# Normalised rows stored as blocks of inner columns, and one instruction for an expert's output rows

## The reference

```python
x = x + gt1[:, None, :] * mix
h2 = modulate(rmsnorm(x, norm2_g[l]), sh2, sc2, dt)          # rows * root * gain + shift
...
def per_sequence(args):
    xs, cw = args
    a = jax.nn.silu(jnp.einsum('sd,edf->sef', xs, w_gate)) * jnp.einsum('sd,edf->sef', xs, w_up)
    return jnp.einsum('sef,efd->sd', a * cw[..., None], w_down)   # cw: two of 32 experts a token
...
x = x + gt2[:, None, :] * ffn
```

## Time and profile before

| | |
|---|---|
| median of 3 runs | 1054.54 us (1052.35 to 1054.55) |
| the profiled execution's own time | 1054.91 us |
| its span | 1053.1 us |
| PE, PEld busy | 979.8 (93%), 768.8 (73%) |
| DVE, ACT busy | 798.3 (76%), 529.1 (50%) |
| L1573, 128x1024, x8 | 1284 ns each |
| L1577, 128x1024, x8 | 1224 ns each |
| `xg_transposes`, L2218 | 256 matmuls |
| `y_evac`, L1795 and L1796 | 32 each, 686 and 677 ns |

### The profile page before, as it was taken

One profiled execution on the slowest core, in us unless ns is written; L12 is line 12 of the kernel. 1 busy time (PEld: TensorE's weight loads), 2 busy tenths in 40 slices (PEclk: granted clock), 3 DMA queues, 4 the chain that ended last, 5 costly groups with the idle time before them and its releaser, 6 DMA issues.

```text
span 1053.1 us, 15470 instructions
## 1 busy us (share of the span) xinstructions
PE 979.8 (93%) x5658; PEld 768.8 (73%) x5658; DVE 798.3 (76%) x1484; ACT 529.1 (50%) x929; POOL 109.4 (10%) x151
## 2 busy tenths in 40 slices
PE   3899988999999999999999999799999999999996
PEld 3668768987897998989988888366666666666642
DVE  8767758944894895967775768888888887777828
ACT  4545432653265465554653333266656656565532
POOL 0200101000100001010000000112211221212100
PEclk9699989999999999999999999899999999999998
DMA  9733423330333225230185434469999999999275
GB/s 365 240 96 119 136 91 91 112 100 22 109 93 101 66 72 164 62 101 1 42 321 185 180 139 182 175 251 367 371 364 366 374 363 359 361 354 347 98 308 210
DMA packets 81033, 206.78 MB, mean 196 GB/s; under 512 B 11878, under 2 KB 40630, under 8 KB 72780
## 3 DMA queue, kind: packets, MB, share of 16 engines
q1 hardware_dynamic: 59232, 156.25, 41.2%
q0 software_dynamic: 15120, 43.72, 13.0%
q10 hardware_dynamic: 6620, 6.00, 1.7%
HBM read 189.61 MB, written 24.71 MB: 204 GB/s over the span
## 4 chain that ended last, share of the span: by engine, by line
PE 60%; DVE 20%; DMA 11%; ACT 4%; issue 4%; SPq 0%; ACTq 0%; DVEq 0%
PE PS L1946 11%; PE PS L1948 10%; PE PS L1947 10%; DMA WGU<-in_w_exp_up 7%; PE PS L2227 4%; DMA AR<-in_w_ada 3%; PE PS L2013 3%; PE PS L2235 3%; PE PS L2234 3%; PE PS L2233 3%; DVE ACC L1253 3%; DVE AT L1427 3%; DVE WL L1318 2%; PE PS L2218 2%; PE PS L2337 1%
## 5 line engine op out<-in xcount | busy, mean ns | idle before, releaser
L1946 PE MATMUL PS<-WH,HT 128*128 128x256 f32 x512 | 147.1, 287 | 1.3 <-ACT GVH L919 1.3
L1947 PE MATMUL PS<-WL,HT 128*128 128x256 f32 x512 | 145.0, 283 | 0.0
L1948 PE MATMUL PS<-WH,HL 128*128 128x256 f32 x512 | 144.9, 283 | 0.0
L1783 DVE TENSOR_TENSOR WGL<-WGU,WGH 128x1024 fp32r<-128x1024 f32 x96 | 116.9, 1220 | 20.1 <-ACT WGH L1161 18.8
L1427 DVE COPY_PREDICATED AT<-MASK,PS 128x64 f32<-128x64 uint8 x320 | 72.7, 227 | 65.9 <-PE PS L2024 47.0
L1161 ACT ACTIVATE WGH<-WGU 128x1024 fp32r<-128x1024 f32 x96 | 98.6, 1064 | 40.5 <-DMA WGU<-in_w_exp_up 32.9
L1946 PEld LDWEIGHTS PS<-WH,HT 128*128 128x128 f32 x512 | 98.4, 192 | 4.0 <-issue 4.0
L1947 PEld LDWEIGHTS PS<-WL,HT 128*128 128x128 f32 x512 | 98.5, 192 | 0.0
L1948 PEld LDWEIGHTS PS<-WH,HL 128*128 128x128 f32 x512 | 98.3, 192 | 0.0
L2233 PE MATMUL PS<-WGH,XGTH 128*96 128x512 f32 x192 | 88.4, 461 | 0.0
L1821 DVE TENSOR_TENSOR WDL<-WDN,WDH 128x2048 fp32r<-128x2048 f32 x32 | 73.4, 2292 | 17.8 <-ACT WDH L1171 17.7
(11 more groups left out here) (349 smaller groups left out, 2248.2 us busy)
## 6 DMA issues: line engine op xcount, KB each, us to landing
WGU<-in_w_exp_gate SPq DMA_DIRECT2D x32, 1024.0 KB, 12.5
WGU<-in_w_exp_up SPq DMA_DIRECT2D x32, 1024.0 KB, 18.6
WDN<-in_w_exp_down SPq DMA_DIRECT2D x32, 1024.0 KB, 14.0
AR<-in_w_ada POOLq DMA_DIRECT2D x32, 512.0 KB, 4.5
WF<-in_w_in SPq DMA_DIRECT2D x28, 512.0 KB, 5.4
AST<-in_w_ada SPq DMA_DIRECT2D x16, 512.0 KB, 9.1
AR<-in_w_ada_final POOLq DMA_DIRECT2D x16, 512.0 KB, 4.4
YG<-expert_rows SPq DMA_DIRECT2D x8, 1024.0 KB, 13.3
```

What stands on the lines that cost most here:

```text
L1783: V.tensor_tensor(WGL[s][:, :, ks, :], WGU[s][:, :, ks, :], WGH[(NCH * s + c) % 4][:].bitcast(F32), ALU.subtract).then_inc(wgl_ready, 1)
L1946: MM(ps, wh, xh, start=first, stop=False)
L1947: MM(ps, wh, xl, start=False, stop=False)
L1948: return MM(ps, wl, xh, start=False, stop=last)
```

## The change

Three edits.

1. `XN` is written in another order of columns. In `rows_scaled` DVE still reads `X1` and `GS2B` contiguously, but writes with the inner dimension `k` at a distance of 128 elements (512 bytes): block `k` of a row then holds columns `k, k + 8, ...` side by side. `rows_shifted` reads and writes `XN` contiguously, and reads `SH2B` at a distance of 8 elements (32 bytes).
2. `xg_transposes` reads `k * P:(k + 1) * P` where it read `k::KD`. The stored and gathered rows have the same sizes, and what lands in PSUM is the same.
3. `y_evac` multiplies both halves in one instruction of 96x1024.

```diff
             def rows_scaled(t):
                 if t >= 2:
                     v_.wait_ge(xn_st[t % 2], 16 * (t // 2))
-                link(V.scalar_tensor_tensor(out=XN[:, t % 2, :], in0=X1[:, t, :], scalar=RR[:, t:t + 1], in1=GS2B[:],
-                                            op0=ALU.mult, op1=ALU.mult))
+                link(V.scalar_tensor_tensor(out=XN[:, t % 2, :].rearrange("p (k n) -> p n k", k=KD),
+                                            in0=X1[:, t, :].rearrange("p (n k) -> p n k", k=KD), scalar=RR[:, t:t + 1],
+                                            in1=GS2B[:].rearrange("p (n k) -> p n k", k=KD), op0=ALU.mult, op1=ALU.mult))
 
             def rows_shifted(t):
-                V.tensor_tensor(XN[:, t % 2, :], XN[:, t % 2, :], SH2B[:], ALU.add).then_inc(xn_ready, 1)
+                xn = XN[:, t % 2, :].rearrange("p (k n) -> p k n", k=KD)
+                V.tensor_tensor(xn, xn, SH2B[:].rearrange("p (n k) -> p k n", k=KD), ALU.add).then_inc(xn_ready, 1)
...
             def y_evac(par, done):
-                V.tensor_tensor(YB[0:C, par, 0:HALF], YP[par][0:C, 0:HALF], GT2B[0:C, 0:HALF], ALU.mult)
-                V.tensor_tensor(YB[0:C, par, HALF:D], YP[par][0:C, HALF:D], GT2B[0:C, HALF:D], ALU.mult).then_inc(done, 1)
+                V.tensor_tensor(halves(YB[0:C, par, :]), halves(YP[par][0:C, :]), halves(GT2B[0:C, :]), ALU.mult).then_inc(done, 1)
...
             def xg_transposes(slot, done):
                 for k in range(KD):
-                    last = TR(TP[:, k // 4, (k % 4) * C:(k % 4 + 1) * C], XG[0:C, slot, k::KD], IDENT[0:C, 0:C])
+                    last = TR(TP[:, k // 4, (k % 4) * C:(k % 4 + 1) * C], XG[0:C, slot, k * P:(k + 1) * P], IDENT[0:C, 0:C])
```

## The result

The changed kernel took 1059.09 us (median of 7 runs, 1057.74 to 1062.76), against 1053.19 us for the kernel before in the same jobs. The ratio is 1.0053, interval 1.0042 to 1.0064: 5.6 us slower (4.4 to 6.7). The profiled execution took 1061.27 us, its span 1059.4 us where it was 1053.1. Of these 6.3 us the first 1.9 are not the change's: `residual` of tile 0, ahead of which no instruction was touched, starts at 596.58 us, where it was 594.69 (in the thirteen traces of this document it starts anywhere from 593.64 to 597.61 us).

The account below looks back on a forecast made before the run. Full DMA load stream bounds the expert stage; PE, then DVE from tile 4, the rows stage. 1054.9 + 4.7 - 0.6 - 0.1 = 1058.9 us, as a median 1058.5, put at 1059.0; 8-in-10 range 1051.5 to 1064.0.

Parts of the forecast that it names:

- Both strides cost: Main case: on DVE the strided write of rows_scaled and strided read of rows_shifted each cost 0.75 us; chance 0.50.
- d: Extra DVE time per tile in the two rows instructions: 1.5 us, with bounds 0 and 2.15 us.
- How d adds up: Rows stage: each residual's delay is the previous one plus d, less DVE's waits, reaching 3.65 us at residual(7).
- The room of DVE: DVE's waits ahead of residual, which absorb delay: 1.84 us in tiles 2 to 4, 0.22 and 0.53 in 6 and 7.
- F: Delay at rows_shifted(7), carried into the start of the full DMA stream: 4.7 us, with bounds 1.5 and 9.9.
- PE's lateness in tile 7: PE's transposes of tile 7 come 3.65 less 0.45 us of room late, 3.20 us, and DVE waits for them.
- The gain in the expert stage: 0.6 us from transposes of the second and fourth sets, plus 0.1 us from merged y_evac in experts 30 and 31.
- The forecast's 0.28 us a step: PE's saving per set of eight contiguous transposes: 8 x 0.027 us from start distances plus 0.065 us.
- Only one stride: Rival: on DVE only the write or only the read costs; F = 1.5, gain 0.7, time 1055.3 us; chance 0.17.
- none: Rival: no stride costs on DVE; time 1053.8 us; chance 0.12.
- PE's saving coming through: Rival: DMAs serve more than 368 GB/s, expert stage ends 8.7 us earlier; time 1050.5 or 1047 us; chance 0.21.
- the stride costs nothing on PE: Rival: transposes save nothing, sum 0.6 us higher, 1059.6 us, not told apart by time; no chance given.

Follow-up runs that it names:

- only the write strided: Changed kernel with the shift row stored in block order beforehand, so rows_shifted is contiguous: ratio 1.0025, 2.6 us slower than the kernel before.
- rows instructions alone: Changed kernel with strided transposes and two y instructions again, leaving only the new rows instructions: ratio 1.0046, 4.9 us slower than the kernel before.
- the buffer given back early: Changed kernel with DVE's copy that frees PE's ranks buffer moved up in one_hots(0): ratio 1.0065 to the kernel before.
- transposes alone: Kernel before with only the transposes made contiguous, rows and y instructions as before: ratio 0.9999.
- one y instruction: Kernel before with only y_evac merged into one instruction: ratio 0.9998.
- two strided reads: Kernel before with rows_scaled writing contiguously and reading X1 and GS2B at 32 bytes: one execution, durations only, 1.02 us more than with no stride.
- 16 bytes: Kernel before with rows_scaled writing and rows_shifted reading the shift row at 16 bytes: one execution, durations only, 2.06 and 2.00 us.
- blocks by ACT: ACT copies X1 into XN in block order, DVE's rows instructions contiguous, transposes and y_evac as in the changed kernel: ratio 0.9996 to the kernel before.
- 8 bytes: Kernel before with rows_scaled writing and rows_shifted reading the shift row at 8 bytes: one execution, durations only, 1.28 and 1.23 us.
- the light pair: Kernel before and changed kernel, both loading only half the down weights of experts 4 to 31: ratios 0.9943 and 0.9927, medians 1048.78 and 1047.36 us.

## Why the prediction was right

**Both strides cost** was the case forecast, and both do. The price was d = 1.5 us a tile from a single row, 0.75 for each instruction. They measured 0.79 and 0.84, and from start of L1573 to the next `residual` a tile takes 4.07 us where it took 2.57 (601.05 - 598.48): 1.50 us, as forecast. That it comes to 1.50 and not to 0.79 + 0.84 is the overlap noted at the first profile lines. That one row of another operation gave it to 0.01 us is partly luck: by starts the write is above 0.75 and the read below. The choice to price the write like the read, for which no row stood, is shown right by the kernel with only the write strided.

**How d adds up.** Forecast for `residual(1)`, (2), (5), (6), (7): 1.5, 1.16, 1.69, 2.97, 3.65 us; measured 1.51, 1.21, 1.86, 3.18, 4.40. The room of DVE in each tile was what counted. The same arithmetic with one stride alone had given F = 1.5, and the kernel with only the write strided shows 1.6.

**The term that was too small is PE's lateness in tile 7.** The forecast let PE's transposes of tile 7 come 3.65 - 0.45 = 3.20 us late, with PE itself on time and at its old pace. They came 4.40 us late, and F was 5.9 us and not 4.7. Two things were left out. The first is a wait. PE had 2.96 us of room for the residual, but next to none for the ranks' buffer in tile 6, which stands behind `one_hots(0)` on the same DVE queue: before the change PE started 0.23 us after that copy ended, and now the transposes of tile 6 come 2.7 us late. The second is PE's pace behind the wait: at a granted clock of 0.64 and 0.51 the matmuls up to tile 7 lose another 1.7 us.

The trace of the rows instructions alone has the first without the second. The wait for the buffer is as long there, the clock stays at 1.00, and `residual(7)` does not wait for PE at all: the transposes of tile 7 come 3.44 us late, close to 3.20. So the wait for the buffer does not cost anything at `residual(7)` by itself; some 0.2 us of the 1.2 are sizes, and the other 1 us is, by this comparison of two traces, the lower clock. The kernels that escape it in tile 6 meet it one step later, in the logits of tile 7 (3.50 us, and 3.60 with the buffer given back early), where DVE waits for them 0.72 and 0.82 us: F is 5.6 in both.

**The gain in the expert stage** was put at 0.6 + 0.1 us. The two traces alone say 1.5, but single traces differ by as much with the same code in the stage (338.4 and 336.5 in the first column). All eleven full-load traces, the stage in us:

| transposes with stride | | contiguous transposes | |
|---|---|---|---|
| before | 338.4 | changed | 336.9 |
| rows alone | 336.2 | transposes alone | 335.9 |
| one y instruction | 337.6 | only the write strided | 338.6 |
| two strided reads | 336.8 | ranks' buffer early | 337.4 |
| 16 bytes | 336.5 | blocks by ACT | 337.2 |
| 8 bytes | 337.7 | | |
| mean | 337.2 | mean | 337.2 |

So the saving there is not to be told from nothing, with 2 to 3 us between traces of either kind, and the 0.7 us can't be confirmed or excluded. That DMAs, and not PE, set the stage's end is shown by the light pair, where the same edit is worth 6.2 us. The forecast's 0.28 us a step was 0.21: the two light kernels take 9.70 and 9.49 us a step. The part from the distance between starts, 8 x 0.027 = 0.22 us, is all that came; the 0.065 us added to it for the weight load did not.

**The sum.** Forecast 4.7 - 0.7 = 4.0 us, with 0.5 us more for the range's lopsidedness; measured 5.6 (4.4 to 6.7), with F at 5.9 in the trace. The 1.2 us that F was short are the larger part of the 1.6 between sum and measurement, and the rest is within the interval. That the median of 1059.09 us falls on the forecast of 1059.0 is luck: the kernel before had a median of 1053.19 in the same jobs, 1.4 us under the one that the forecast started from, and this made up for the term that was too small.

**Rivals.** Only one stride, none, and PE's saving coming through are excluded by the durations and by the transposes alone. That the stride costs nothing on PE is wrong as well (0.21 us a set), but as the forecast said, the time doesn't show it. One sign that the forecast had named against itself did appear: GB/s above 370 after 720 us, 372 and 377 in the changed kernel. The bound was set too close. The kernel before itself has 371 between 790 and 820 us, and at 372 and 377 GB/s PE still ran short of weights from the stretch after 820 us on, earlier than the 860 us named. The figure of 358 GB/s that the forecast sets beside the stretches is thus passed by about 5%. DVE's room in the expert stage is 3.6 to 6.2 us of 30 by the earlier trace rows, not 3 to 5; nothing hangs on it.

**Open.** Why the stage differs by 2 to 3 us between traces at DMA shares of 0.98 to 1.02 was not looked into. Nor is it shown why the clock fell in tile 6 behind a wait of 2.22 us in the changed kernel (and of 2.25 in its light version), and stayed at 1.00 behind one of 2.24 in the kernel with the rows instructions alone. In each of these traces the fall came behind waits of PE; no run tried the waits by themselves.

## What to carry to other kernels

Ask of a saving which stage it falls in and what that stage waits for: 0.2 us a step on an engine that is busy 100% was worth nothing that runs can show, because a queue with a growing latency stood behind it, and 6 us as soon as that queue had room. Put a stride where an engine waits anyway: the reordering cost about 5 us on DVE and nothing that runs can show on ACT. When a delay meets another engine, list everything that engine waits for at that point, buffers given back included, and allow for a slower engine behind a new wait: here the wait itself was harmless, and the lower clock behind it cost 1 us.

## What was not expected of the hardware

A float32 stream of DVE pays a fixed step between 8 and 16 bytes of stride (1.28 to 2.06 us for a write of 1024 elements, 1.23 to 2.00 for a read) and hardly more up to 512 bytes (2.08); a second strided stream adds 0.2 us. ACT seems to pay too: a copy of 512 elements written at 512 bytes takes 1.13 us, its squares of 512 contiguous elements, another operation, 0.63 us. PE's loads of 96x128 weights fell from 207 to 140 ns without the stride, and sets of eight transposes from 1.02 to 0.82 us. Behind waits of 0.5 to 2.2 us in a busy row of float32 matmuls the granted clock fell to 0.50 for some microseconds: the matmuls started 0.42 us apart instead of 0.23, and 16 small ones took 3.5 us instead of 1.95. It did not fall behind every such wait (2.24 us idle, and 1.00 after it).
